# One quarter of one down chunk computed as three float32r products in a mixture-of-experts loop

## The reference

```python
gu = xb @ w_gate_up[e] + b_gate_up[e]                # [rows, 1024] x [1024, 2048]
gate = jnp.minimum(gu[:, :D_EXPERT], SWIGLU_LIMIT)
up = jnp.clip(gu[:, D_EXPERT:], -SWIGLU_LIMIT, SWIGLU_LIMIT)
glu = gate * jax.nn.sigmoid(SWIGLU_ALPHA * gate)
y = ((up + 1.0) * glu) @ w_down[e] + b_down[e]        # [rows, 1024] x [1024, 1024]
```

## Time and profile before

| | |
|---|---|
| median of 2 runs | 2092.57 us (2090.02 to 2095.12) |
| the profiled execution's own time | 2084.95 us |
| its span | 2083.2 us, granted clock 0.998 |
| PE busy | 2058.3 us, 99% of the span |
| gate and up products, L2247 | 667.9 us |
| down products, L2261 | 337.8 us |
| single-pass products of the dense parts, L396 to L398 | 1011.3 us in six groups |
| DVE / ACT / POOL busy | 41% / 22% / 18% |

### The profile page before, as it was taken

One profiled execution on the slowest core, in us unless ns is written; L12 is line 12 of the kernel. 1 busy time (PEld: TensorE's weight loads), 2 busy tenths in 40 slices (PEclk: granted clock), 3 DMA queues, 4 the chain that ended last, 5 costly groups with the idle time before them and its releaser, 6 DMA issues.

```text
span 2083.2 us, 42388 instructions
## 1 busy us (share of the span) xinstructions
PE 2058.3 (99%) x17798; PEld 1260.8 (61%) x17798; DVE 859.9 (41%) x1468; ACT 455.7 (22%) x741; POOL 369.3 (18%) x413
## 2 busy tenths in 40 slices
PE   9999999999999999999999999999999999999999
PEld 6888877343443443443443443447786788888887
DVE  4554435433333333333333333324665443443544
ACT  4151432000000000000000000023554532212211
POOL 2010001113223223223223223221202400000000
PEclk9999999999999999999999999999999999999999
DMA  7334126999999999999999999973111022322231
GB/s 263 101 115 139 61 74 248 381 398 406 409 413 408 408 413 409 408 413 410 401 413 408 408 412 404 408 287 117 61 62 41 1 81 70 112 81 101 86 101 55
DMA packets 141117, 520.14 MB, mean 250 GB/s; under 512 B 16300, under 2 KB 71896, under 8 KB 91808
## 3 DMA queue, kind: packets, MB, share of 16 engines
q1 hardware_dynamic: 120384, 495.02, 60.2%
q0 software_dynamic: 20672, 24.26, 4.9%
HBM read 509.09 MB, written 18.88 MB: 253 GB/s over the span
## 4 chain that ended last, share of the span: by engine, by line
PE 78%; DMA 2%; ACT 1%; DVE 1%; issue 0%; POOL 0%; POOLq 0%; DVEq 0%; ACTq 0%
PE ps L2247 31%; PE ps L2261 15%; PE ps L396 8%; PE ps L398 8%; PE ps L397 8%; DMA ring<-in_w_gate_up 1%; PE ps L2055 1%; PE ps L2049 1%; PE ps L2112 1%; PE ps L2075 1%; PE ps L2005 1%; PE ps L2142 1%; PE ps L498 1%; PE ps L2037 0%; PE ps L1961 0%; DMA xg<-h_rows,idx 0%
## 5 line engine op out<-in xcount | busy, mean ns | idle before, releaser
L2247 PE MATMUL ps<-ring,xe 128*32 128x512 f32 x6144 | 667.9, 592 | 1.4 <-DVE xe L1681 0.9
L2247 PEld LDWEIGHTS ps<-ring,xe 128*32 128x32 f32 x6144 | 202.8, 110 | 422.5 <-issue 410.1
L2261 PE MATMUL ps<-ring,act_t 128*32 128x256 f32 x6144 | 337.8, 379 | 1.4 <-DVE act_t L1674 1.2
L2261 PEld LDWEIGHTS ps<-ring,act_t 128*32 128x32 f32 x6144 | 206.6, 110 | 139.9 <-issue 18.7
L396 PE MATMUL ps<-xt_hi,hi 128*128 128x512 f32 x544 | 213.6, 393 | 0.8 <-DVE ff_a L1735 0.8
L398 PE MATMUL ps<-xt_hi,lo 128*128 128x512 f32 x544 | 211.8, 389 | 0.0
L397 PE MATMUL ps<-xt_lo,hi 128*128 128x512 f32 x544 | 211.7, 389 | 0.0
L1140 ACT ACTIVATE glu<-glu 128x768 f32<-128x768 f32 x32 | 27.0, 843 | 633.5 <-DVE glu L1688 633.5
L790 POOL DMA_INDIRECT x_rows<-ye,idx x96 | 152.7, 1591 | 38.0 <-issue 38.0
L1655 DVE COPY idx<-idx 128x3 int32<-128x3 int32 x33 | 5.6, 169 | 354.3 <-DMA x_rows<-ye,idx 347.2
L383 DVE TENSOR_TENSOR lo<-raw,hi 128x2048 fp32r<-128x2048 f32 x44 | 101.4, 2310 | 92.4 <-ACT hi L376 85.5
(11 more groups left out here) (339 smaller groups left out, 2471.2 us busy)
## 6 DMA issues: line engine op xcount, KB each, us to landing
ring<-in_w_gate_up SPq DMA_DIRECT2D x256, 1024.0 KB, 19.0
ring<-in_w_down SPq DMA_DIRECT2D x128, 1024.0 KB, 20.0
raw<-in_w_in SPq DMA_DIRECT2D x20, 1024.0 KB, 6.4
raw<-in_w_gate SPq DMA_DIRECT2D x11, 1024.0 KB, 5.4
raw<-in_w_up SPq DMA_DIRECT2D x11, 1024.0 KB, 5.3
raw<-in_w_down SPq DMA_DIRECT2D x11, 1024.0 KB, 4.9
raw<-in_w_out SPq DMA_DIRECT2D x8, 1024.0 KB, 5.1
raw<-in_w_k SPq DMA_DIRECT2D x4, 1024.0 KB, 5.1
```

What stands on the lines that cost most here:

```text
L2247: last = pe.matmul(ps[QUAD * j:QUAD * j + QUAD, g, :], xe[:, g, QUAD * k:QUAD * k + QUAD], w[:, j, :, :], start=k == 0, stop=k == KT - 1)
L2261: last = pe.matmul(y_block(g, j, bank), act_t[:, g, QUAD * (2 * c + h):QUAD * (2 * c + h) + QUAD], w[:, h, QF * j:QF * j + QF], start=c == ...
```

## The change

For down chunk 2 (`SPLIT`) of each expert in the loop, tile 0's quarter of the columns is no longer multiplied natively. ScalarE writes the rounded weights of that quarter (`w_top`, 128x512) and of the activations that meet this chunk (`a_top`, 128x192) as float32r; VectorE writes the remainders, the weights' in place over the quarter in the ring slot (`w_rest`), the activations' to `a_rest`. TensorE runs three float32r products of 256 columns for that quarter in place of one native one. Tiles 1 to 3 keep their native products of the same chunk. The other three down chunks, the gate and up chunks, and the last expert's down product behind the loop stay as they were. A few semaphores outside the loop are merged (two waits each on one count), which adds and removes no wait.

```diff
+            act_cols = act_t[:, :, 2 * QUAD * SPLIT:2 * QUAD * SPLIT + 2 * QUAD]
+            def quarter_top(n):
+                act.wait_ge(m_raw[4 + SPLIT], n * 16 + 32)
+                act.wait_ge(m_used, n * 12 + 8)
+                act.activation(w_top[:, :, :], m_slot(4 + SPLIT).rearrange("p (h c) -> p h c", h=2)[:, :, 0:QF], ACT.Copy)
+                act.wait_ge(m_at, n + 1)
+                act.activation(a_top[:, :, :], act_cols, ACT.Copy).then_inc(m_split, 1)
...
                 bias_evacuate(i + 1)
+                quarter_top(i)
                 gate(i + 1)
...
+            def quarter_rest(n):
+                dve.wait_ge(m_split, n * 2 + 1)
+                w = m_slot(4 + SPLIT).rearrange("p (h c) -> p h c", h=2)[:, :, 0:QF]
+                dve.tensor_tensor(w_rest[:, :, 0:QF], w, w_top[:, :, :].bitcast(F32), ALU.subtract)
+                dve.tensor_tensor(a_rest[:, :, :], act_t[:, :, 2 * QUAD * SPLIT:2 * QUAD * SPLIT + 2 * QUAD],
+                                  a_top[:, :, :].bitcast(F32), ALU.subtract).then_inc(m_split, 1)
...
                 indices(i + 2, i * 48 + 16, i * 48 + 96)
+                quarter_rest(i)
                 swiglu(i + 1, i * 12 + 16)
...
+            def down_chunk_split(c, q, n, bank=3):
+                pe.wait_ge(m_split, n * 2 + 2)
+                w = m_slot(q).rearrange("p (k n) -> p k n", k=2)
+                for h in range(2):
+                    for g in range(GROUPS):
+                        y0 = y_block(g, 0, bank)
+                        top, rest = (a[:, g, QUAD * h:QUAD * h + QUAD] for a in (a_top, a_rest))
+                        pe.matmul(y0, top, w_top[:, h, :], start=False, stop=False, skip_group_check=True)
+                        for j in range(1, 4):
+                            pe.matmul(y_block(g, j, bank), act_t[:, g, QUAD * (2 * c + h):QUAD * (2 * c + h) + QUAD],
+                                      w[:, h, QF * j:QF * j + QF], start=False, stop=False, skip_group_check=True)
+                        pe.matmul(y0, rest, w_top[:, h, :], start=False, stop=False, skip_group_check=True)
+                        last = pe.matmul(y0, top, w_rest[:, h, 0:QF], start=False, stop=False, skip_group_check=True)
+                last.then_inc(m_used, 1)
...
                 for c in range(4):
-                    down_chunk(c, 4 + c, i * 16 + 32)
+                    if c == SPLIT:
+                        down_chunk_split(c, 4 + c, i)
+                    else:
+                        down_chunk(c, 4 + c, i * 16 + 32)
```

More of the change, by code:

```diff
@@ L34 @@
 RING, KEEP, REST = 12, 4, 12
+RING_ORDER = (2, 0, 1, 5, 8, 3, 6, 4, 7, 11, 12, 13, 14, 9, 10, 15)
+SPLIT = 2
 SPAN = SEQ + P
@@ L194, in program @@
         bias_b = at("bias_b", K(8), [P, 2 * QF])
+        w_top = at("w_top", K(31.75), [P, 2, QF], F32R)
+        a_top = at("a_top", K(33.75), [P, GROUPS, 2 * QUAD], F32R)
+        a_rest = at("a_rest", K(34.5), [P, GROUPS, 2 * QUAD], F32R)
+        w_rest = at("w_rest", 8 * KB * RING_ORDER[4 + SPLIT], [P, 2, D], F32R)
         wT = at("wT", K(52), [NE, SEQ])
@@ L321, in program @@
         moe_dve_step = sem("moe_dve_step")
-        r_in, r_wlo, r_done, r_sub, r_exp, r_mask, r_pos, r_wt, r_wt_sb = (sem(f"route_{s}") for s in
-            ("inputs", "weights_split", "logits_done", "shifted", "exp", "masks", "positions",
+        r_in, r_wsplit, r_done, r_sub, r_exp, r_mask, r_pos, r_wt, r_wt_sb = (sem(f"route_{s}") for s in
+            ("inputs", "weights_hi_then_lo", "logits_done", "shifted", "exp", "masks", "positions",
              "weightsT", "weightsT_sb"))
         r_lgT, r_lgT_sb = sem("route_logitsT"), sem("route_logitsT_sb")
-        r_hi, r_table = sem("route_w_hi"), sem("route_tables")
+        r_table = sem("route_tables")
         b_in, b_top, b_left = sem("bias_loaded"), sem("bias_bf16_part"), sem("bias_remainder")
@@ L335, in program @@
             ("bias", "bias_sb", "bias_added", "glu", "act", "act_transposed"))
+        m_split = sem("m_quarter_rounded_then_remainder")
         m_y, m_scat, xg_zero, held = (sem(s) for s in ("m_y", "m_scattered", "xg_zero", "m_held"))
@@ L339, in program @@
             ("bias", "squares", "rstd", "x"))
-        rel_dma, rel_flip, rel_f, rel_fs, lam_s, lam_e = (sem(f"rel_{s}") for s in
-            ("dma", "turned", "f", "f_sb", "lambda_sums", "lambda_exp"))
+        rel_dma, rel_flip, rel_f, rel_fs, lam_s = (sem(f"rel_{s}") for s in
+            ("dma", "turned", "f", "f_sb", "lambda_sums_then_exp"))
         hn_sq, hn_ss, hn_var, hn_rstd = (sem(f"head_norm_{s}") for s in ("squares", "sums", "variance", "rstd"))
@@ L573, in m_slot @@
         def m_slot(s):
-            return ring[:, (2, 0, 1, 5, 8, 3, 6, 4, 7, 11, 12, 13, 14, 9, 10, 15)[s], :]
+            return ring[:, RING_ORDER[s], :]
         def moe_load(sp, e, j, q):
@@ L954, in scalar_program @@
             act.wait_ge(r_in, 16)
-            copy(wr_hi, wr[:, :, :]).then_inc(r_hi, 1)
+            copy(wr_hi, wr[:, :, :]).then_inc(r_wsplit, 1)
             norm_behind_chunk("ffn", SA, A_END - 1, logits=True)
@@ L965, in scalar_program @@
             act.wait_ge(lam_s, 1)
-            act.activation(tiny[:, 42:44], tiny[:, 40:42], ACT.Exp).then_inc(lam_e, 1)
+            act.activation(tiny[:, 42:44], tiny[:, 40:42], ACT.Exp).then_inc(lam_s, 1)
             hi_part(act, SB, 0)
@@ L1350, in vector_program @@
                               ALU.subtract).then_inc(b_left, 1)
-            dve.wait_ge(r_hi, 1)
-            dve.tensor_tensor(wr_lo, wr[:, :, :], wr_hi.bitcast(F32), ALU.subtract).then_inc(r_wlo, 1)
+            dve.wait_ge(r_wsplit, 1)
+            dve.tensor_tensor(wr_lo, wr[:, :, :], wr_hi.bitcast(F32), ALU.subtract).then_inc(r_wsplit, 1)
             dve.wait_ge(gain_in[1], 32)
@@ L1362, in vector_program @@
                 s.then_inc(lam_s, 1) if i else link(s)
-            dve.wait_ge(lam_e, 1)
+            dve.wait_ge(lam_s, 2)
             link(dve.tensor_tensor(tiny[:, 44:45], tiny[:, 43:44], tiny[:, 42:43], ALU.subtract))
@@ L2147, in router_logits @@
             evacuated(pe, SA, SA.first[A_END - 1] + t)
-            pe.wait_ge(r_wlo, 1)
+            pe.wait_ge(r_wsplit, 2)
             o = logits_bank(t)
```

## The result

| | before | after |
|---|---|---|
| median of 2 runs | 2092.57 us (2090.02 to 2095.12) | 2200.49 us (2197.47 to 2203.51) |
| profiled execution's own time | 2084.95 us | 2197.47 us |
| its span, granted clock | 2083.2 us, 0.998 | 2195.7 us, 0.999 |

The ratio is 1.0516, 95% interval 1.0433 to 1.0599: slower by 5%, 108 us. The forecast was 2200, in a range of 2146 to 2236.

What follows compares the result with a forecast made beforehand. PE alone bounds the kernel, at 31.24 us a trip. Products 1.98 plus switches 1.68 make 3.66 us over 31 trips: 2084.95 + 113.5 - 0.6 = 2198, or 2206 from the median; forecast 2200 us, range 2146 to 2236.

Steps and rivals of the forecast that it cites:

- The float32r products exclude the tiles: In down chunk 2, TensorE's float32r products run between the tiles' bursts, not beside them; 3.66 us a trip with switches.
- Rival 1: In down chunk 2 float32r products run beside the tiles, so not slower: about 2089 us, chance 0.11.
- The switch price: Each change between tiles and float32r products in down chunk 2 costs 0.12 us; 14 a trip, 1.68 us.
- Rival 2: Float32r products exclude the tiles but switches are free: 31 x 1.98 = 61 us, 2146, chance 0.05.
- rival 4: Dearer switches in down chunk 2, 0.20 us each: 148 us, 2233; chance of that or more 0.02.
- The product price: Each float32r product in down chunk 2 takes 0.11 us with the tiles idle; 18 a trip, 1.98 us.
- The sum: TensorE's added 3.66 us a trip over 31 trips, 113.5 us, less 0.6 of waits: 2198 us.
- The base: Time the additions start from: profiled execution 2084.95 us, giving 2198; from the median 2092.57, 2206.
- the cover: VectorE's added subtractions, 0.65 and 0.25 us, fit its idle stretch of 2.14 us before L1688, costing nothing.
- PE's 0.6 us of waits for DMA: TensorE's waits for loads in the last trips, 0.6 us in all, would disappear with the longer trip.
- The loads: In the loop, `in_w_down` landings return to about 7 to 10 us, with a DMA share of about 0.92.
- Tiles 1 to 3 still need their two rounds: Removing tile 0's native products from down chunk 2 saves nothing: the other tiles still take 0.43 us a group.

Runs made afterwards that it cites:

- e1: Changed kernel with chunk 2's 18 float32r products in one run behind all native ones: 2154.53 us, ratio 1.0304 to the kernel before.
- e3: Changed kernel, same order, with the rounded and remainder parts in bf16 instead of float32r: 2090.57 us, ratio 0.9993 to the kernel before.
- e6: Kernel before plus six tiny float32r products of fixed operands in down chunk 2, into an unused PSUM bank: 2144.35 us, ratio 1.0250.
- e7: Kernel before plus six tiny products of fixed operands in down chunk 2, as bf16: 2096.99 us, ratio 1.0026.
- e9: Kernel before plus one tiny float32r product of fixed operands ahead of down chunk 2 each trip: 2101.66 us, ratio 1.0055.
- e2: Changed kernel with the splitting and waits kept, but TensorE multiplying all four quarters natively: 2092.53 us, ratio 1.0005 to the kernel before.
- e8: Kernel before with every native down product in the loop replaced by three bf16 products of fixed operands: 2085.00 us, ratio 0.9970.
- e4: Changed kernel with its float32r products 64 columns wide instead of 256: 2155.77 us, ratio 1.0310 to the kernel before.
- e5: The kernel before, unchanged, profiled once more: 2089.86 us, one run.
- e10: Kernel before plus three bf16 products of 224 columns on each of four tiles at the head of down chunk 2: 2099.90 us, ratio 1.0048.

## Why the prediction was right, and where its sizes were off

**The float32r products exclude the tiles.** The forecast rested on the router's products and on L2279, against the plain reading that an output of 32 partitions stays in its tile. Both rows were indirect: L2151 and L2153 write overlapping partitions, and no row shows whether they would overlap in time if they did not, and L2279 is a transpose. The runs show it directly: e1 (order alone is worth some 45 us, 108 less 63), e3 (the type alone decides) and e6 against e7. What they show is that a float32r product doesn't run beside native products in other tiles. Whether four float32r products in four tiles would run side by side no run tests; here all are tile 0's. The same idle products cost 53 us as float32r and 6 as bf16 (e6, e7). Rival 1 was the bf16 kernel's story: 2090.57 us (e3).

**The switch price.** Taken at 0.12 us from three gaps of 0.11 and one of 0.20; measured 0.127 by e1; 14 of them are 1.78 us a trip, 55 us in all, nearly half of the loss. The 0.01 over the gaps stood for the first round's wait for its weights, an estimate: no run shows that wait apart from the gap. Rival 2 (no switches, 2146) and rival 4 (0.20, 2233) fall with it.

**The product price.** Taken at 0.11 from the earlier trace rows, measured 0.116 by e1: 18 are 2.10 us a trip, 65 us. That a native record passes over its columns twice is the author's reading of two times, 0.430 us against 0.22 for a bf16 record of the same 512 columns; the trace shows no passes.

**The sum.** The trip grew by 3.87 us, where the forecast had 3.66 with both prices a little low: 35.11 and not 34.9, chunk 2 6.32 and not 6.2. 31 x 3.87 = 120 us instead of 113.5. That 1.78 + 2.10 gives the 3.87 back is no test, since the prices were solved from it; the test is e6, 1.70 expected with them and 1.71 found. The range's upper end of 2236 stands 3 us above the 2233 that it is said to hold, without a working.

**The base.** That the number came out within 1 us was luck: two errors met, and 2200 was picked between the sums 2198 and 2206. The term was 6.5 us short. And the sum was made against an execution of 2084.95 us without the 0.3 us a trip that ordinary executions lose, and from the median it was 2206; the changed kernel does not have that loss, so from the median the account would be, by the estimate of 9 us above, 2092.6 + 120 - 9 = 2203.6 against 2200.5 measured. Between the two profiled executions the loop grew by 118.4 us (120 less 0.5 that the trips of before lose and 1.0 in the stretch ahead of the first full trip), and the stages outside it became 5.9 us shorter: 112.5 in all, own time to own time. 3.3 of the 5.9 us lie behind the loop, and nearly all of them at one place: before has a granted clock of 0.50 from 1597.5 to 1604 us, after has no such stretch there, and the hundred records around it take 27.8 us against 24.7. The other 2.6 lie ahead of the loop: at the start four products of 512 columns take 3.78 us before and 1.98 after. The trace of before has no record of the clock in its first 13.6 us, so that a low clock is the reason there is not shown. A stretch like the one at 1597 isn't the change's doing as far as the profiles tell: e1 and e3, which split the quarter too, have it, and e9, which doesn't, has none.

**What was costed at nothing.** ScalarE's and VectorE's additions measured 0.63 + 0.35 and 0.69 + 0.35 us a trip where 0.9 each was forecast; the cover held (5.63 us idle behind them), and e2 shows that they cost nothing even with the late loads of before. PE's 0.6 us of waits for DMA went, as forecast.

**The loads.** Landings fell to 7 us, as forecast (7 to 10). The DMA share in the loop is 0.97 and not 0.92: the share is not proportional to the bytes moved, for 374 GB/s are 9% less than 410, and the share fell by 5%. Nothing in the sum hung on it.

**No gain to be had.** "Tiles 1 to 3 still need their two rounds" is e1's L2299 row (2.59 us without tile 0) and e3's 0.43 us a group. e8 adds what the forecast had not said: the loads would have capped a better version too.

## What to carry to other kernels

Before a product is swapped for a cheaper kind inside a set of column tiles, look at whether that kind exists in the tiles at all: find a place in the trace where both kinds meet and read the gap from start to start. Where they exclude each other, the changes between them can cost nearly as much as the work (1.78 against 2.10 us a trip here), so put all of the one kind in one run. And time a profiled execution against the median before making a sum on it: here the kernel before had one with a loop some 6 us shorter than when it was profiled again.

## What the runs showed of the hardware

- A float32r product with 32 stationary columns and an output of 32 partitions doesn't run beside native float32 products in the other column tiles (e1, e6); a bf16 one does (e3, e7). A change between such products and the tiles costs 0.127 us each way on average with 32-wide weights, whichever PSUM bank is written and however short the product (e1, e4, e6); the one reading behind 128-wide work, back to the tiles, is 0.20 us.
- Six excursions of 0.03 us of work each cost 1.71 us a trip (e6); the same as bf16 cost 0.14 to 0.19 (e7).
- With PE's work in the down product cut by a quarter, loads at 411 GB/s held the kernel within 0.3% of its time (e8).
- Two profiled executions of the same program, 2084.95 and 2089.86 us, differ in trips of 31.26 and 31.51 us on average, with no wait in the profile that explains it.
- The four column tiles need not keep in step, and products in different tiles can start out of program order: in e5 a bias product starts at 841.29 us, behind gate and up products that the program has after it (from 841.10); in the earlier trace rows's execution the four start together. The time doesn't go by this: e9, in step, and e10, out of step, take 2101.66 and 2099.90 us.
